# The modulation spread and the context decay sums as products of two rounded parts, in a two-block network kernel on one core

## The reference, cut to what matters

```
sh1, sc1, g1, sh2, sc2, g2 = [m[:, None, :] for m in _adaln(c, w_mod[i], b_mod[i])]   # silu(cond) @ w_mod + b_mod
hc = _rmsnorm(ctx, norm1_g[i]) * (1 + csc1) + csh1
uc, qc, kc, vc, lfc, lbc, gc, gtc = _project(hc, *proj_params)
st_f = _gla_final_state(kc, vc, lfc)              # cum = cumsum(log_a); k_rem = k * exp(cum[-1] - cum); k_rem^T v
st_b = _gla_final_state(_flip(kc), _flip(vc), _flip(lbc))
hx = _rmsnorm(x, norm1_g[i]) * (1 + sc1) + sh1
ux, qx, kx, vx, lfx, lbx, gx, gtx = _project(hx, *proj_params)
ox = _gla_bidirectional(qx, kx, vx, lfx, lbx, st_f, st_b)
x = x + g1 * _mixer_out(pooled_x, ox, gx, gtx, *mix_params)
x = x + g2 * _hier_moe(_rmsnorm(x, norm2_g[i]) * (1 + sc2) + sh2, *moe_params)
```

## Time and profile before

| | us |
|---|---|
| median of the runs | 1346.62 |
| the profiled execution | 1345.76 |
| its span | 1343.7 |
| mixer from 60 to 175 us: TensorE busy | 114.35 of 115 |
| the same: VectorE busy | 98.03 |
| the same: ScalarE busy | 48.41 |
| the same: GpSimd busy | 0.00 |
| experts, 370 to 740 us: moved by the DMA engines | 428 GB/s |

### The profile page before, as it was taken

How to read it: one execution, slowest core, us unless ns; L and a number is a source line. 1 busy time by engine, 2 the same in 40 slices (tenths; PEclk the granted TensorE clock), 3 DMA queues, 4 the chain that set the end, 5 groups by cost and what they waited for, 6 DMA issues and landing times.

```text
span 1343.7 us, 21991 instructions
## 1 busy us (share of the span) xinstructions
PE 1178.9 (88%) x9307; PEld 918.4 (68%) x9307; DVE 690.2 (51%) x1045; ACT 482.3 (36%) x691; POOL 0.2 (0%) x4
## 2 busy tenths in 40 slices
PE   5999999998876757567676899999999999999997
PEld 4678888886543424234343799878888899888886
DVE  3688857775211101011110577586666767766666
ACT  5552346544110100000000454554444456544443
POOL 0000000000000000000000000000000000000000
PEclk9999999999997988788898999999999999999999
DMA  9968576689999999999999764435545344463620
GB/s 342 342 223 277 190 297 250 219 322 379 423 426 429 428 428 427 426 428 429 428 428 425 296 250 155 160 114 199 207 169 212 119 158 178 167 232 144 239 75 32
DMA packets 89130, 371.94 MB, mean 277 GB/s; under 512 B 6506, under 2 KB 8344, under 8 KB 76380
## 3 DMA queue, kind: packets, MB, share of 16 engines
q1 hardware_dynamic: 87496, 369.73, 70.3%
q10 hardware_dynamic: 1556, 1.08, 0.3%
HBM read 369.74 MB, written 1.05 MB: 276 GB/s over the span
## 4 chain that ended last, share of the span: by engine, by line
PE 70%; DMA 22%; DVE 4%; ACT 2%; issue 2%; SPq 1%; DVEq 0%; ACTq 0%
DMA arena<-in_moe_w 20%; PE ring L2060 8%; PE ring L2498 7%; PE ring L2049 5%; PE acc L2149 5%; PE acc L2150 4%; PE acc L2151 4%; PE ring L2062 4%; PE ring L2051 2%; PE acc L2033 2%; PE acc L2035 2%; PE acc L2034 2%; DMA arena<-in_w_mod 1%; PE ring L2197 1%; PE ring L2199 1%
## 5 line engine op out<-in xcount | busy, mean ns | idle before, releaser
L2498 PE MATMUL ring<-arena 128*32 128x256 f32 x2048 | 149.5, 456 | 73.3 <-DMA arena<-in_moe_w 72.5
L2498 PEld LDWEIGHTS ring<-arena 128*32 128x32 f32 x2048 | 78.0, 130 | 140.4 <-issue 70.2
L1287 DVE TENSOR_TENSOR wlo<-arena,whi 128x2048 fp32r<-128x2048 f32 x56 | 128.0, 2290 | 50.1 <-ACT whi L847 50.1
L1730 DVE TENSOR_TENSOR arena<-arena,ring 128x128 f32<-128x128 f32 x32 | 12.1, 379 | 253.5 <-ACT arena L1091 253.5
L1091 ACT ACTIVATE arena<-ring 128x128 f32<-128x128 f32 x32 | 8.9, 277 | 344.3 <-PE ring L2498 344.3
L847 ACT ACTIVATE whi<-arena 128x2048 fp32r<-128x2048 f32 x56 | 106.8, 1910 | 43.1 <-PE acc L2151 25.4
L2060 PE MATMUL ring<-xboth,whi 128*128 128x512 f32 x320 | 113.8, 398 | 0.0
L2062 PE MATMUL ring<-xboth,wlo 128*128 128x256 f32 x320 | 89.8, 281 | 0.0
L2060 PEld LDWEIGHTS ring<-xboth,whi 128*128 128x128 f32 x320 | 60.1, 188 | 14.6
L2049 PE MATMUL ring<-hboth,w1hi 128*128 128x512 f32 x192 | 68.6, 401 | 0.1
L2527 PE MATMUL acc<-above 32*128 32x256 f32 x512 | 45.7, 425 | 25.0 <-DVE above L1737 18.2
(11 more groups left out here) (419 smaller groups left out, 2656.4 us busy)
## 6 DMA issues: line engine op xcount, KB each, us to landing
arena<-in_moe_w SPq DMA_DIRECT2D x79, 2048.0 KB, 20.6
arena<-in_mlp_w_in SPq DMA_DIRECT2D x16, 2048.0 KB, 10.2
arena<-in_mlp_w_out SPq DMA_DIRECT2D x16, 2048.0 KB, 7.9
own<-in_moe_w SPq DMA_DIRECT2D x15, 2048.0 KB, 25.0
arena<-in_w_in SPq DMA_DIRECT2D x10, 2048.0 KB, 8.7
arena<-in_w_mod SPq DMA_DIRECT2D x7, 2048.0 KB, 14.3
arena<-in_moba_w_qkv SPq DMA_DIRECT2D x6, 2048.0 KB, 19.5
own<-in_w_mod SPq DMA_DIRECT2D x4, 2048.0 KB, 10.9
```

What stands on the lines that cost most here:

```text
L1287: dve.tensor_tensor(lo, raw, hi.bitcast(F32), ALU.subtract).then_inc(G["split_ready"], 1)
L2498: ins = pe.matmul(o, xs[:, kt, j, :], w[kt][g], start=(kt == 0), stop=(kt == KT - 1))
```

## The change

Six edits, made together:

1. Spread s is two fp32r products with a rounded matrix of ones (`ones_r`), one of the high part and one of the low part of `mod_part`. GpSimd makes both parts: a copy that rounds (`mod_high`, one buffer) and a subtraction (`mod_low`, in the place of `mod_part`).
2. The context decay sums are fp32r products of two parts too: ScalarE rounds the log-gates (`L_high`, 2 pieces of 128x1024), GpSimd subtracts (`L_low`, 2 pieces) and rounds the three matrices (`sums_r`). 6 float32 products become 12 fp32r ones.
3. The bias is added before the spread. SyncE brings only one row of 4 KB per vector, onto partition 0 of a buffer that GpSimd has set to zero, and the first block of each slab sum is a scalar_tensor_tensor that adds that buffer. The four row transfers stand behind the slabs mod 4 and mod 5.
4. The spread's result is read from PSUM by ScalarE (a copy), no longer by VectorE.
5. Slab w_in 4 comes in two transfers of 1 MB, and `pre_hi(6)` waits for the first only.
6. The pool weights, whose place `mod_high` now uses, are loaded behind w_in 7 and after spread 11, no longer at mod 6.

```diff
+        mod_high = split_at("mod_high", 45 * K1, 512)
+        mod_low = [split_at(f"mod_low{b}", 44 * K1 + 512 * b, 512) for b in range(2)]
+        L_high = split_at("L_high", 32 * K1, 4, DK)
+        L_low = split_at("L_low", 24 * K1 + 4 * DK, 4, DK)
+        sums_r = split_at("sums_r", 36 * K1, 3, P)
 ...
-                if (name, s) == ("mod", 4):
-                    sp.wait_ge(G["h_ready"], KT)
-                    for j, dst in enumerate((bc_g1, bc_sh2, bc_gain2, bc_g2)):
-                        spread(dst, a["b_mod"][0][(2 + j) * D:(3 + j) * D], bc_in)
-                if (name, s) == ("mod", 6):
+                if (name, s) == ("w_in", 1):
+                    sp.wait_ge(G["bc_zero"], 4)
+                    for j, dst in enumerate((bc_gain2, bc_g2, bc_g1, bc_sh2)):
+                        r = (4, 5, 2, 3)[j] * D
+                        sp.dma_start(dst[0:1, :], a["b_mod"][0][r:r + D].unsqueeze(0)).then_inc(bc_in, 16)
+                if (name, s) == ("w_in", 8):
+                    sp.wait_ge(bank_full, BANK_AT["mod_bc", 11] + 1)
                     sp.dma_start(w_pool[:, :, :], a["pool_w"][0].rearrange("g c e -> c g e")).then_inc(pool_in, 16)
...
+        @block.gpsimd
+        def _(pool):
+            for dst in (bc_gain2, bc_g2):
+                pool.memset(dst, 0.0).then_inc(G["bc_zero"], 1)
+            pool.wait_ge(G["h_ready"], KT)
+            for dst in (bc_g1, bc_sh2):
+                pool.memset(dst, 0.0).then_inc(G["bc_zero"], 1)
...
+            for d in range(2):
+                v = slice(2 * d, 2 * d + 2)
+                pool.wait_ge(G["L_hi_ready"], d + 1)
+                pool.tensor_tensor(L_low[:, v, :], L[:, 4 + 2 * d:6 + 2 * d, :], L_high[:, v, :].bitcast(F32), ALU.subtract).then_inc(G["L_lo_ready"], 1)
+            for s in range(4, 12):
+                part = mod_part[:, s % 2, :]
+                pool.wait_ge(G["part_ready"], KT * (s - 3))
+                if s > 4:
+                    pool.wait_ge(bank_full, BANK_AT["mod_bc", s - 1] + 1)
+                pool.tensor_copy(mod_high, part).then_inc(G["part_high"], 1)
+                pool.wait_ge(G["part_high"], s - 3)
+                pool.tensor_tensor(mod_low[s % 2], part, mod_high.bitcast(F32), ALU.subtract).then_inc(G["part_low"], 1)
...
-                        ins = dve.tensor_scalar(part, w[:, kt, :], scale, None, ALU.mult)
+                        if s == 4:
+                            dve.wait_ge(bc_in, 16 * 4)
+                        ins = dve.scalar_tensor_tensor(part, w[:, kt, :], scale, spread_row(s), ALU.mult, ALU.add)
...
-                pe.wait_ge(G["part_ready"], KT * (s - 3))
-                full(pe.matmul(b, ones, mod_part[:, s % 2, :], start=True, stop=True))
+                pe.wait_ge(G["part_high"], s - 3)
+                pe.matmul(b, ones_r[:, :], mod_high, start=True, stop=False)
+                pe.wait_ge(G["part_low"], s - 3)
+                full(pe.matmul(b, ones_r[:, :], mod_low[s % 2], start=False, stop=True))
```

More of the change, by code:

```diff
@@ L801, in _, with spread_row @@
             sp.wait_ge(G["out_stored"], 16 * 4)
+        def spread_row(s):
+            return (bc_g1, bc_sh2, bc_gain2, bc_g2)[s // 2 - 2][:, 512 * (s % 2):512 * (s % 2) + 512]
+        @block.gpsimd
[5 more added lines that the diff above has]
+                pool.memset(dst, 0.0).then_inc(G["bc_zero"], 1)
+            pool.wait_ge(consts_in, 16)
+            pool.tensor_copy(ones_r[:, :], ones).then_inc(G["rounded"], 1)
+            pool.wait_ge(bank_full, BANK_AT["z", (1, 3)] + 1)
+            for i, name in enumerate(("suf", "pre", "all")):
+                pool.tensor_copy(sums_r[:, i, :], C(name)).then_inc(G["rounded"], 1)
+            for d in range(2):
[10 more added lines that the diff above has]
+                pool.tensor_tensor(mod_low[s % 2], part, mod_high.bitcast(F32), ALU.subtract).then_inc(G["part_low"], 1)
         @block.scalar
@@ L853, in pre_hi @@
                     act.wait_ge(keys_half_in, 16)
+                elif PRE[i] == ("w_in", 4, 0):
+                    act.wait_ge(values_half_in, 16)
                 else:
@@ L932, in _ @@
             value_tokens(0)
+            for d in range(2):
+                act.wait_ge(G["L_ready"], 3 + d)
+                act.activation(L_high[:, 2 * d:2 * d + 2, :], L[:, 4 + 2 * d:6 + 2 * d, :], ACT.Copy).then_inc(G["L_hi_ready"], 1)
             value_tokens(1)
@@ L947, in _ @@
             pre_hi(5)
+            mod_bc(5)
             pre_hi(6)
@@ L2273, in _ @@
                 b = bank("remc", i)
+                pe.wait_ge(G["L_hi_ready"], d + 1)
+                pe.wait_ge(G["L_lo_ready"], d + 1)
                 other = (d == 0 and tt == 0) or (d == 1 and tt == 1)
-                ins = pe.matmul(b, C(("suf", "pre")[d]), L[:, 4 + 2 * d + tt, :], start=True, stop=not other)
+                parts = (L_high[:, 2 * d + tt, :], L_low[:, 2 * d + tt, :])
+                pe.matmul(b, sums_r[:, d, :], parts[0], start=True, stop=False)
+                ins = pe.matmul(b, sums_r[:, d, :], parts[1], start=False, stop=not other)
                 if other:
-                    ins = pe.matmul(b, C("all"), L[:, 4 + 2 * d + 1 - tt, :], start=False, stop=True)
+                    pe.matmul(b, sums_r[:, 2, :], L_high[:, 2 * d + 1 - tt, :], start=False, stop=False)
+                    ins = pe.matmul(b, sums_r[:, 2, :], L_low[:, 2 * d + 1 - tt, :], start=False, stop=True)
                 full(ins)
```

47 lines of the change are left out of this document (23 added, 24 removed).

## The result

The changed kernel takes 1349.61 us (median of 16 runs, 1348.03 to 1351.61), the kernel before 1346.53 beside it (16 runs). The ratio is 1.0021, its 95% interval 1.0015 to 1.0028: 3.1 us slower, where 4.3 us less were forecast. The profiled execution took 1351.15, its span 1349.4; it lies 1.5 above its median.

The account below looks back on a forecast made before the run. The prediction took TensorE to bound the mixer, with VectorE the bound near the queries and v 4. 1.9 us by v 4 plus 2.4 from six spreads gave 4.3 us less, 1342.3; own range 1341 to 1344, overall 1340.5 to 1351.

Parts of the forecast that it names:

- TensorE's products: In the mixer, spreads save 0.40 us each (eight, 3.2) and decay sums 2.4: 5.6 us as an upper bound.
- the decay sums ended as forecast: On TensorE before spread 4, the last decay sum ends at 82.0 instead of 83.87, 1.85 us earlier.
- the experts passed the difference on: The byte-bound expert stage starts its loads earlier with the mixer, so the mixer's gain reaches the total time.
- GpSimd's parts ... Cost: nothing: `L_low` and the spreads' pairs on GpSimd are ready in time, with 1.2 us over at spread 4; cost nothing.
- rival A: GpSimd blocks VectorE's two-SBUF-input work at 75 to 93 us, 4.7 to 8.4 us; total +0.7 to +6, named 1351; chance 0.27.
- VectorE before the queries: The pinch: `pre_lo(4)` ends at 95.0, TensorE waits 1.2 us, queries start at 95.0 instead of 96.4; 1.4 us gained.
- the v 4 of the forecast: Behind the queries, the stall before v 4 vanishes; v 4 starts at 106.75 instead of 108.66, 1.9 us earlier.
- Forecast 2.4 from six spreads: Behind v 4, spreads 6 to 11 save 0.40 us each on TensorE, 2.4 us together.
- Rival B: GpSimd is slow without blocking, so low parts come late before spread 4: 1346.1, no change; chance 0.20 shared with another rival.

Follow-up runs that it names:

- e7: Changed kernel with the spreads as float32 products again, GpSimd making only the log-gates' low parts and the rounded matrices: 1349.30 us, ratio 1.0026 to the kernel before.
- e3: Changed kernel with the decay sums float32 again, without `L_high` and `L_low`; GpSimd keeps the pairs for the spreads: 1344.73 us, ratio 0.9983 to the kernel before.
- e2: Kernel before, with GpSimd only writing (memsets into an unused place) at the moments of its work in the changed kernel: 1346.97 us, ratio 1.0001.
- e9: Changed kernel with `L_low` made by VectorE and slab sums 6 and 7 cut and reordered around the low parts: 1347.62 us, ratio 1.0006 to the kernel before.
- e4: Changed kernel with VectorE reordered: `pre_lo(4)` ahead of slab sum 6, slab sums 6 and 7 cut in halves: 1346.72 us, ratio 1.0004 to the kernel before.
- e1: Kernel before, with GpSimd doing the changed kernel's copies and subtractions at the same moments on constants, results unused: 1351.54 us, ratio 1.0036.
- e8: Changed kernel with float32 decay sums, `pre_lo(4)` ahead of slab sum 6, slab sum 7's second half behind `pre_lo(7)`: 1346.51 us, ratio 1.0002 to the kernel before.
- e10: Changed kernel with float32 decay sums, slab sum 6 left in place and slab sum 7 cut into two, four and two steps: 1342.83 us, ratio 0.9970 to the kernel before.
- e5: Changed kernel with `L_low` made by VectorE between slab sums 4 and 5 instead of by GpSimd: 1347.40 us, ratio 1.0008 to the kernel before.
- e6: Changed kernel with spreads and decay sums both float32 products again, the other four edits kept: 1346.07 us, ratio 0.9998 to the kernel before.
- e11: Changed kernel with float32 decay sums and slab w_in 4 in one transfer of 2 MB: 1343.66 us, ratio 0.9977 to the kernel before.

## Why the prediction was wrong, step by step

**Right: TensorE's products and ScalarE's part.** The spread's products are 0.23 apart in pairs. Spread 4 started at 82.15, so the decay sums ended as forecast (82.0); its second product came at 82.60, because GpSimd had the low part ready at 82.54 only (forecast 80.8), and v 2 started at 82.94 (82.5), 0.3 later than two products behind 82.15. TensorE was done with v 2, v 3 and spread 5 at 94.4 (forecast 93.8), 2.0 ahead of before. ScalarE's reads of the spreads, the bias rows and the pool weights caused no wait, and the experts passed the difference on.

**Wrong: "GpSimd's parts ... Cost: nothing".** This step asked only when the parts are ready, and that was nearly right: the wait for them cost 0.3 us. It did not charge VectorE. The charge stands in rival A, which got a chance of 0.27, because the trace of before was silent. Measured, slab sum 5 lost 5.2 us beyond the 0.27 of edit 3; the two `L_low` pieces took 4.1 of it (two steps in 5.6 us instead of 1.5; in e7, where they are alone, 4.0) and the pair of spread 4 the rest (1.0 in e3). The pair of spread 5 fell beside the decay copies and key products and cost at most 0.3. Rival A had counted the key products among what has two inputs in SBUF, and charged this pair with 1.2 to 1.9; one of their inputs is in PSUM, and they lost nothing. `pre_lo(4)` ended at 100.0, forecast 95.0. The step "VectorE before the queries" fell with it; its pinch was the right place.

**Missing: the price of a wait.** Neither the forecast nor rival A had TensorE's clock as a term. The queries took 12.9 us instead of 11.6. With the 5.0 late of `pre_lo(4)` that makes 6.3, which is the distance between the v 4 of the forecast (106.75) and the one measured (112.99).

**Nearly right: behind v 4.** Forecast 2.4 from six spreads; from v 4 to the pool product the lead of the kernel before shrinks from 4.3 to 2.5, which is 1.8, and at the router 1.2 are left. Of the 0.6 that are missing up to the pool product, about half comes before the first state, where a shorter spread 7 no longer covers ScalarE's read of v 7 (135.48 to 136.08) and TensorE waits 0.2 for its bank; the other half I have not found. The last 0.6, between the pool product and the router, need not be the change's: that stretch takes 123.56 us in the kernel before, 124.19 in the changed one, 122.80 in e3 with the same instructions as the changed one, and 124.29 in e2 with the same TensorE instructions as the kernel before. What sets it isn't settled.

**Rival A by its numbers.** It had +0.7 to +6 and named 1351; 1349.6 is inside. It gave v 4 at 111.7 to 116.1 (measured 113.0), and the wait it asked for was 6 us or more, measured 5.7. It was right by lock and place, at a blocking of some 5.5 us out of 4.7 to 8.4. That its sum comes out is in part luck: it left out the clock (1.3 us) and charged the pair of spread 5 with 1.2 to 1.9 where 0.3 came. Rival B did not happen here, but e9 shows that it exists, as the other side of A and not as a slow GpSimd: 1.28 us for a subtraction of 512 columns undisturbed. The order alone was not at fault: reordering (e4) brought 2.9 back and left the kernel where it had been before the change.

**Not settled:** the low clock between 305 and 320 us. It is there for 7 us in the profiles of the changed kernel and of e7, for 3.4 us in those of e1, e4, e8 and e10, and not in those of the kernel before, e2, e3, e5, e6, e9 and e11; no wait of more than 0.5 us stands right ahead of it, only the router's small products. By the start of the rank products the long one costs 2.5 us and the short one 0.8 (from the router on 12.4 and 10.7 us, where the kernel before takes 9.9). It can also come elsewhere: the profile of e3 is 2.5 ahead of the kernel before at 727 us and 0.4 at 779, and its clock stood at 0.50 from about 739 to 742, which that of the kernel before did not; e11, which is as far ahead at 779 as at the router, has no such place. One profile a kernel doesn't say how often this happens. Where it does, it is as large as much of what the variants differ by, so a difference of the times of 1 to 2 us between two of them is to be trusted only with the starts in the mixer beside it.

## What to carry to other kernels

Before work is given to an idle GpSimd, look at what VectorE does in the same stretch, not at how idle GpSimd is: if VectorE is a bound there and works on two inputs in SBUF, GpSimd's reading instructions are charged to it. The two subtractions of 128x1024 were charged nearly in full (4.1 us), a pair of 128x512 with about half of its 1.9 us (1.0), and the same work may be cheaper on VectorE itself (2.35 us against 4.1). Zeroing on GpSimd cost nothing that could be measured. Charge a wait of TensorE of 2 us or more with the products at half clock behind it as well (1.3 us more for the queries of the changed kernel, 2.3 in e7), and after each reordering look for the next engine that waits at the next place: of the four orders tried (e4, e8, e9, e10) only the one that moved a single slab sum into existing idle time ended ahead of the kernel before.

## What the runs showed of the hardware

- GpSimd and VectorE excluded each other by whole instructions, in turns, where GpSimd read SBUF and VectorE had two inputs there (a step of 0.75 us became 2.8 us), and a tensor_scalar with one SBUF input was shut out as well (0.48 became 2.58 us in e1). Beside memsets the same tensor_scalar took 0.66. A tensor_tensor with one input in SBUF and one in PSUM was not touched (four in 2.48 us, with GpSimd's subtraction beside them and without).
- GpSimd undisturbed: rounding copy of 128x512 0.61 us, subtraction 1.27 to 1.30; two subtractions of 128x1024 with one VectorE step between them 5.64 (of this up to 0.6 is a wait for the VectorE step under way at their start).
- After each wait of 2.15 us or more in the mixer (2.15, 3.8, 3.9, 4.1, 5.7, and the 2.7 in e9 that follows one of 1.8 with a single product between) TensorE ran at 1.2 GHz (granted clock 0.50) for 3 to 6 us, from its first product on or, in e1, from 1 us behind it; after those of 0.6 to 1.4 in the mixer it stayed at 2.4 GHz (1.00).
